# Down products of three dense feed-forwards by seven block products instead of eight, with the sums on VectorE

## What is computed

```python
# first block, for each of 2 layers, behind three kinds of attention:
h2 = rms_norm(x, ln2_g[l])
ff = square(relu(h2 @ w_ff1[l]))          # D_FF = 4096
x = x + ff @ w_ff2[l]                     # "down": 256 x 4096 times 4096 x 1024

# second block, for each of 2 layers:
mod = silu(c) @ ada_w[l] + ada_b[l]       # six rows of 1024: shift, scale, gate, twice
...
h = rms_norm(x, ffn_norm_g[l]) * (1 + scale_f) + shift_f
# layer 0, dense, D_FF_2 = 2816; layer 1 is a mixture of 8 experts instead
y = (silu(h @ w_gate) * (h @ w_up)) @ w_down
x = x + gate_f * y
```

## Time and profile before

| | |
|---|---|
| median of 3 runs | 2496.72 us |
| span of the profiled execution | 2499.3 us |
| its own time | not given apart from the span |
| PE busy | 2440.1 us, 98% |
| DVE, ACT, POOL busy | 651.3, 418.3, 53.8 us |
| read from HBM | 614.69 MB, 246 GB/s over the span |
| granted clock of TensorE, mean | 0.993 of 2.4 GHz |

### The profile page before, as it was taken

One profiled execution on the slowest core, in us unless ns is written; L12 is line 12 of the kernel. 1 busy time (PEld: TensorE's weight loads), 2 busy tenths in 40 slices (PEclk: granted clock), 3 DMA queues, 4 the chain that ended last, 5 costly groups with the idle time before them and its releaser, 6 DMA issues.

```text
span 2499.3 us, 27928 instructions
## 1 busy us (share of the span) xinstructions
PE 2440.1 (98%) x11210; PEld 1540.3 (62%) x11211; DVE 651.3 (26%) x1441; ACT 418.3 (17%) x1052; POOL 53.8 (2%) x110
## 2 busy tenths in 40 slices
PE   9999999999999999999999999988999989999998
PEld 6666466656565566676777756547996544445444
DVE  0453210011543134455244362101002101011101
ACT  1243010010441132211113112101001101010101
POOL 0000000000000000000000000000000000000000
PEclk9999999999999999999999999998999999999999
DMA  6323344334232688444667458998567999779971
GB/s 263 122 102 126 109 169 168 140 119 157 102 113 106 241 304 312 184 157 169 249 286 303 158 220 362 426 425 368 219 277 300 427 426 426 317 303 425 426 293 80
DMA packets 78971, 617.33 MB, mean 247 GB/s; under 512 B 5984, under 2 KB 6112, under 8 KB 39184
## 3 DMA queue, kind: packets, MB, share of 16 engines
q1 hardware_dynamic: 73920, 558.39, 56.0%
q0 software_dynamic: 4656, 56.47, 5.8%
q10 hardware_dynamic: 288, 0.90, 0.1%
HBM read 614.69 MB, written 1.05 MB: 246 GB/s over the span
## 4 chain that ended last, share of the span: by engine, by line
PE 91%; DMA 5%; DVE 2%; issue 1%; POOL 0%; ACT 0%; SPq 0%; DVEq 0%; POOLq 0%; ACTq 0%
PE G L2160 9%; PE S L2485 8%; PE S L2487 8%; PE G L1883 6%; PE G L1925 5%; DMA big<-in_moe_pack 4%; PE S L2153 4%; PE T L2153 4%; PE G L2501 4%; PE G L2499 4%; PE G L2107 3%; PE S L2371 3%; PE T L2371 3%; PE G L2394 3%; PE S L2553 2%; PE G L2223 2%
## 5 line engine op out<-in xcount | busy, mean ns | idle before, releaser
L2485 PE MATMUL S<-big,hT 128*64 128x256 f32 x2240 | 270.7, 384 | 27.2 <-DMA big<-in_moe_pack 25.6
L2485 PEld LDWEIGHTS S<-big,hT 128*64 128x64 f32 x2240 | 158.4, 137 | 136.6 <-issue 54.3
L2160 PE MATMUL G<-big 128*128 128x512 f32 x512 | 222.2, 592 | 0.0
L1781 DVE TENSOR_TENSOR probs<-S,probs 128x128 f32<-128x128 f32 (+2 forms) x105 | 35.5, 338 | 680.3 <-ACT probs L1100 680.1
L2487 PE MATMUL S<-big,hT 128*128 128x512 f32 x448 | 201.3, 593 | 2.1 <-issue 2.1
L1925 PE MATMUL G<-big,hT 128*128 128x384 f32 x512 | 171.0, 488 | 0.0
L2160 PEld LDWEIGHTS G<-big 128*128 128x128 f32 x512 | 97.2, 190 | 116.0 <-issue 115.3
L1883 PE MATMUL G<-big,hT 128*128 128x372 f32 x512 | 160.8, 476 | 0.4 <-DMA big<-in_proj_pack 0.4
L2487 PEld LDWEIGHTS S<-big,hT 128*128 128x128 f32 x448 | 82.8, 190 | 96.5 <-issue 96.5
L1883 PEld LDWEIGHTS G<-big,hT 128*128 128x128 f32 x512 | 97.0, 190 | 63.4 <-DMA big<-in_proj_pack 1.0
L1925 PEld LDWEIGHTS G<-big,hT 128*128 128x128 f32 x512 | 95.8, 190 | 65.3 <-issue 4.0
(11 more groups left out here) (363 smaller groups left out, 2735.2 us busy)
## 6 DMA issues: line engine op xcount, KB each, us to landing
big<-in_moe_pack SPq DMA_DIRECT2D x112, 2048.0 KB, 15.7
big<-in_moe_pack SPq DMA_DIRECT2D x112, 1024.0 KB, 17.5
big<-in_w_ff SPq DMA_DIRECT2D x32, 2048.0 KB, 8.5
big<-in_ada_pack POOLq DMA_DIRECT2D x24, 2048.0 KB, 14.1
big<-in_ffn_pack SPq DMA_DIRECT2D x11, 3072.0 KB, 14.5
big<-in_gate_pack SPq DMA_DIRECT2D x16, 1536.0 KB, 6.3
big<-in_proj_pack SPq DMA_DIRECT2D x15, 1488.0 KB, 6.2
big<-in_branch_heads SPq DMA_DIRECT2D x6, 2048.0 KB, 7.9
```

The lines of the kernel that those rows point to most:

```text
L2160: return mm(G[j][:, :], hid[:, c % 2, f, b * P:(b + 1) * P], w[:, f, half * 512:(half + 1) * 512], start=(c == 0 and f == 0), stop=(c == 7 ...
L2485: ins = mm(S[s % 2][f * FEW:(f + 1) * FEW, 0:SEQ], hTe[:, k, 0:FEW], wt[:, k, f * SEQ:(f + 1) * SEQ], start=(k == 0), stop=(k == KD - 1))
```

## The change

The core of the diff:

```diff
-QUARTERS = ((0, 1, 2, 3), (0, 2, 1, 3))
+PRODUCTS = (1, 2, 3, 5, 7, 6, 4)
+LAST_PRODUCTS = ((1, 2, 6, 7, 4, 5, 3), (1, 2, 6, 5, 3, 7, 4))
...
+        P7 = {1: G[0], 2: T[1], 3: S[1], 4: S[0], 5: G[3], 6: G[1], 7: G[2]}
...
+        def up_bank(c, f):
+            return (T[0] if c else H4[f])[:, 0:SEQ]
...
+        def ffn_bank(n, f, piece):
+            return H4[2 * f + piece][:, 0:SEQ] if n == 0 else T[0][:, piece * SEQ:(piece + 1) * SEQ]
...
@@ DVE, first block
+                def hidden_sums(c):
+                    h = hid[:, c % 2]
+                    a11, a12, a21, a22 = h[:, 0:2, 0:P], h[:, 2:4, 0:P], h[:, 0:2, P:], h[:, 2:4, P:]
+                    dve.wait_ge(ff_ev.sem, ff_ev.at(l, 4 * c + 4))
+                    dve.tensor_tensor(s3, a11, a21, ALU.subtract).then_inc(sums_ok.sem, 1)
+                    dve.tensor_tensor(s1, a21, a22, ALU.add).then_inc(sums_ok.sem, 1)
...
+                def weight_sums(c):
...
+                    dve.tensor_tensor(w_t1, w12, w11, ALU.subtract).then_inc(sums_ok.sem, 1)
+                    dve.wait_ge(sums_ok.sem, summed(l, c, "t1"))
+                    dve.tensor_tensor(w12, w22, w12, ALU.subtract).then_inc(sums_ok.sem, 1)
+                    dve.tensor_tensor(w_t2, w22, w_t1, ALU.subtract).then_inc(sums_ok.sem, 1)
+                    dve.wait_ge(sums_ok.sem, summed(l, c, "t2"))
+                    dve.tensor_tensor(w_t4, w21, w_t2, ALU.subtract).then_inc(sums_ok.sem, 1)
                 for j in range(8):
                     for f in range(4):
+                        square(j, f)
+                    if j:
+                        dve.wait_ge(used[(23 + 2 * j) % NSLOT].sem, used_at(l, 23 + 2 * j))
+                    hidden_sums(j)
+                    weight_sums(j)
                     if l == DEPTH - 1:
                         for c in ADA_SLOTS[0][j]:
                             ada(0, c)
...
@@ DVE, second block
+                def step_sums(n):
...
+                    dve.wait_ge(fhid_ok.sem, (n + 1) * FT + FT)
+                    if n:
+                        dve.wait_ge(down_mm.sem, n)
...
+                    dve.tensor_tensor(w, w, bcast(gateB[1].unsqueeze(1), [P, FT, D]), ALU.mult).then_inc(sums_ok.sem, 1)
...
@@ PE, first block
                     for f in range(4):
-                        pe.wait_ge(ff_relu.sem, ff_relu.at(l, 4 * c + f + 1))
+                        pe.wait_ge(ff_relu.sem, ff_relu.at(l, 4 * c + f + (4 if c else 1)))
                         up_part(c, f, KH if c == 0 else 0, KD).then_inc((ff_mm if f < 3 else used[2 * c % NSLOT]).sem, 1)
-                    for d in (c,) if c < 6 else (6,) if c == 7 else ():
-                        weights(l, 25 + 2 * d)
...
+                        if c:
+                            if f == 0:
+                                weights(l, 23 + 2 * c)
+                            for i in PRODUCTS[2 * f:2 * f + 2]:
+                                ins = down_product(c - 1, i)
+                    if c:
+                        ins.then_inc(used[(23 + 2 * c) % NSLOT].sem, 1)
...
@@ PE, second block
+                    for n in range(1, FSTEPS):
+                        pe.wait_ge(arrived_in[(n + 1) % 2].sem, (n // 2 + 1) * 16)
                         for f in range(FT):
-                            pe.wait_ge(fhid_ok.sem, n * FT + (f + 1 + FT))
-                            for j in range(4):
-                                ins = down_piece(n, f, j)
+                            pe.wait_ge(fhid_ok.sem, n * FT + f + FT)
+                            for piece in range(2):
+                                up_piece2(n, piece, f, 0, SEQ).then_inc((fg_mm, fu_mm)[piece].sem, 1)
+                            if (n, f) == (1, 0):
+                                pe.wait_ge(gateB_ok.sem, gateB_ok.at(l, 4))
+                            for i in PRODUCTS[4 * f:4 * f + 4]:
+                                ins = down_product(n - 1, i)
                         ins.then_inc(down_mm.sem, 1)
```

More of the change, by code:

```diff
@@ L1552, in _, with done, grow @@
-                if l == 0:
-                    turned_pair(l * 2 + 2, 3, xn_turned, T[1], hT_dve, gainc[l + 1][0])
+                def done(i):
+                    if i == LAST_PRODUCTS[l][-1]:
+                        dve.wait_ge(used[39 % NSLOT].sem, used_at(l, 39))
+                    else:
+                        dve.wait_ge(ff2_mm.sem, ff2_mm.at(l, LAST_PRODUCTS[l].index(i) + 1))
+                def grow(half, b, src):
+                    xs = x[:, b, half * 512:(half + 1) * 512]
+                    return dve.scalar_tensor_tensor(out=xs, in0=src, scalar=small[:, 306 + b:307 + b], in1=xs, op0=ALU.mult, op1=ALU.add)
@@ L2193, in _ @@
                         turn_pair(1, x, T[1], xn_turned)
-                    for f in range(4):
-                        ins = down_part(7, f, j)
-                    ins.then_inc((ff2_mm if i < 3 else used[39 % NSLOT]).sem, 1)
+                    down_product(7, i).then_inc((used[39 % NSLOT] if i == LAST_PRODUCTS[l][-1] else ff2_mm).sem, 1)
             def gate_sums(l, part):
@@ L2385, in up_step @@
                     for piece in range(2):
                         for f in range(FT):
[L2387 to L2395 removed]
+                            pe.wait_ge(fhid_ok.sem, f + 1)
@@ new lines, in first_step, with down_product @@
+                            up_piece2(0, piece, f, 0, P)
+                        if piece == 0:
+                            second_block()
+                    second_ready()
+                    for piece in range(2):
+                        for f in range(FT):
+                            up_piece2(0, piece, f, P, SEQ).then_inc((fg_mm, fu_mm)[piece].sem, 1)
+                def down_product(n, i):
+                    h = ffhid[:, n % 2]
+                    w = ffn_slot((n + 1) % 2)[1]
+                    left = {1: h[:, 0, 0:P], 2: h[:, 1, 0:P], 3: fs4, 4: h[:, 1, P:], 5: fs1, 6: fs2, 7: fs3}[i]
+                    right = {1: w[:, 0, 0:512], 2: w[:, 1, 0:512], 3: w[:, 1, 512:], 4: f_t4, 5: f_t1, 6: f_t2, 7: w[:, 0, 512:]}[i]
+                    pe.wait_ge(sums_ok.sem, summed2(n, {1: "wg", 2: "wg", 3: "wg", 4: "t4", 5: "t1", 6: "t2", 7: "t3"}[i]))
+                    return mm(P7[i][:, :], left, right, start=(n == 0), stop=(n == FSTEPS - 1))
@@ new lines, in _ @@
+                            for piece in range(2):
+                                up_piece2(n, piece, f, 0, SEQ).then_inc((fg_mm, fu_mm)[piece].sem, 1)
[3 more added lines that the diff above has]
+                                ins = down_product(n - 1, i)
+                        ins.then_inc(down_mm.sem, 1)
+                    for i in LAST_PRODUCTS[1]:
+                        down_product(FSTEPS - 1, i).then_inc((down_mm if i == LAST_PRODUCTS[1][-1] else ff2_mm).sem, 1)
```

222 lines of the change are left out of this document (140 added, 82 removed).

## The result

| | before | after |
|---|---|---|
| median | 2497.38 us, 4 runs | 2653.35 us, 4 runs |
| range | 2496.67 to 2498.78 | 2650.36 to 2655.56 |
| span of the profiled execution | 2499.3 us | 2652.1 us |
| mean granted clock | 0.993 | 0.963 |

The ratio is 1.0623 (95% interval 1.0608 to 1.0638): 156 us, or 6.2%, slower. The forecast was 2638 us in a range of 2605 to 2668. The spans differ by 152.8 us. In each execution for which both are given the device time is 1.8 to 1.9 us above the span; by that the execution of before behind the earlier trace rows took some 2501 us, 3.8 above its median, and the profiled one of the changed kernel, 2653.96 us, stood 0.6 above its own; the difference of 3.2 us is the rest of the 156.

A forecast was written before the change was run, and what follows sets the result against it. The prediction took TensorE (PE) to bound the kernel. Products -36.9, transfers +89.1, relu waits +42.8, clock +28.6 and ends +17.9 sum to +141.5 us; 2496.7 + 141.5 = 2638 us, range 2605 to 2668.

The forecast's parts named there:

- PE bounds the kernel, and a product off it comes off the time: In the feed-forwards of both blocks, 43 products removed were to take off 36.9 us, all on the path.
- Transfers, 89.1: Second block: steps 2 to 10 wait for the whole weight transfer, nine times 9.9 us, +89.1 us (87 to 131).
- the rival with 14.6 us a wait: Second block: ada's transfers slip beside SP's, so each of nine waits is 14.6 us; 2681 us, chance 0.08.
- Relu behind ada, 42.8: First block, layer 1: four iterations idle PE while ACT's relu stands behind ada's sums, +42.8 us (40 to 46).
- Clock, 28.6: The granted clock falls in each of the 13 new waits and costs 2.2 us each, +28.6 us.
- The light clock term (0.12): Rival: half the forecast's clock loss or less behind the 13 waits, about 2622 us, chance 0.12.
- Ends, 17.9: Ends of both first-block layers and the second block: DVE's sums and x updates without PE work beside them, +17.9 us.
- Nothing else moves: Outside the named terms no time changes, 0 us; w_ff loads keep a 25.7 us iteration for 8 to 20 us.
- Both rivals with one wait alone: Only the second block's transfer wait, 2586 us, chance 0.05; or only layer 1's relu wait, 2529 us, chance 0.03.
- The faster case: Rival: transfer and relu waits both lie beside PE work, only products and ends count; 2478 us, chance 0.03.

The follow-up runs named there:

- Experiment one: Changed kernel with the second block's 3 MB transfer split, its 2 MB of up columns issued an iteration earlier: 2601.99 us, ratio 1.0416.
- Experiments two: Changed kernel with ACT's row sums of ada in layer 1 moved behind the next chunk's first and second relu: 2602.46 us, ratio 1.0411.
- experiment three: Changed kernel with 11 unused products on PE before each wait for a transfer in the second block: 2630.27 us, ratio 1.0528.
- fourth experiment: Changed kernel with DVE doing ada in layer 1 before its wait for PE and the eight sums: 2631.62 us, ratio 1.0531.

## Why the prediction was right, point by point

*PE bounds the kernel, and a product off it comes off the time.* Right. Where the waits were taken away the products' gain shows: layer 1 in 216.8 us instead of 223.8, and layer 0 came out 10.8 us shorter in the changed kernel itself.

*Transfers, 89.1.* Right in mechanism and size: nine waits of 10.1 us for 9.9. The pieces took 9.7 to 10.33 us. POOL issued ada's transfer at 1254.23, 12.2 us after SP's and behind its landing, as I had worked out, and the rival with 14.6 us a wait is out. Experiment one shows the release as the cause.

*Relu behind ada, 42.8.* Right: 42.1. The first came 11.47 us for 11.6, the others 10.2 on average for 10.4. Experiments two and four show the queue of ACT as the cause, with the arithmetic of DVE's part: 7 us earlier ada, 7 us less wait.

*Clock, 28.6.* Right in mechanism, and shown by experiment three: the clock fell behind all thirteen waits. That the sum came out to the tenth is luck: I had picked 2.2 us between 1.7 and 2.5, and single falls cost 1.6 to 3.0. What I had not priced is that PE takes 0.25 us to get going again behind any wait, 3.3 us in all. The light clock term (0.12) is out. The Trainium skill, "TensorE: Matmul & The Clock Gate", section "HAM oscillation — how this bites in real kernels", names the pattern, and this trace agrees with it; by an estimate from its figure the term would have been 11 us, and the rows say 2.6 times that. I also reckoned falls behind the thirteen long waits alone, and so missed those at the ends.

*Ends, 17.9.* This is the term most off: 22.1 us (2.9, 8.1 and 11.1 for 4.0, 5.3 and 8.6). Layer 0 was cheaper. The other two lose the clock besides: the chain of the changed kernel at the end of the second block,

```profile
1534.45 2.21 DVE big L1800
...
1536.70 2.08 PE G L2548 x2
...
1547.75 0.76 DVE rot L1200
...
1548.55 1.67 PE T L2369 x8
```

has two matmul records in 2.08 us, where two take 0.86 at full clock, and eight small ones in 1.67 for 0.87. Half-clock stretches of 3.4 us at the end of layer 1 and of 6.8 and 3.4 at that of the second block, up to 6.8 us lost, can carry the whole 5.3 us by which these two ends were over.

*Nothing else moves.* Wrong by two moves that nearly cancel: some 6 us more in the mixture of experts, 5.0 of them the second stop, and some 3 us less at 2050 to 2060 us. The mixture's half-clock stretch of the earlier trace rows was 23.9 us instead of 17.1, but most of what it grew by lies in the stop, where PE idles and loses nothing by the clock. The 3.0 us left over are small by chance.

*From profile to median.* I added differences to 2496.7, where the profiled execution, by the 1.8 us around a span, stood some 4 above its median. Of the 15 us between forecast and result, these make some 4, PE's restarts 3.3, the ends 4.2, elsewhere 3.0 and the two waits 0.8.

*The range.* 2605 to 2668 does not follow from the bounds that I named for it. 5.1 us a fall and 27 us of ends add 47 us to the forecast, and 0 and 9 take 37 off: 2601 to 2685. The result, 15 us above the forecast, lies in both.

Both rivals with one wait alone are answered by experiments one and two: each mended alone left the kernel 103 us over before. The faster case needed both covered, and with both covered the kernel was faster, 2490 us where I had 2478.

## What to carry to other kernels

When a consumer is moved later in an engine's order, its release moves with it: look at what that increment lets go, and at what stands next on the same engine. A merged loop that gives up PSUM banks takes away the slack that an engine queue with side work had lived on; put the side work behind the operations that others wait for. A saving of products on TensorE is worth what its sums cost where nothing covers them, at the ends, so it pays with many chunks (8 of 16 products) and not with small steps. Before a difference of a few us between two programs is put down to an edit, it should be looked up by stage: here 5 us came and went behind everything that was edited.

## What was not expected of the hardware

Idle stretches of TensorE of 2.93 to 2.99 us were followed by half clock in five of six cases, where I had reckoned only with long ones. In the fourth experiment the same followed all three of 2.86 us, both of 3.01, and one of 1.87 us (behind it eight records of 512 columns took 2.67 and 2.93 us, four and four, for the 1.98 and 1.88 that they take behind the same wait in the changed kernel); idle of 0.56 to 0.61 us never was followed by it. Unused products in an otherwise idle wait were worth 20 us over nine waits, and cost 1.4 us of longer waits. And a stop of TensorE of about 5 us, some 300 us behind the last edited instruction, is there in six of the nine programs and not in the other three, with half clock around it for 20.5 or 23.9 us instead of 17.0.
